# A hybrid encoder block on one core: the input projection spread over the steps of attention and mLSTM, and attention's scores with keys on partitions

## The chip, the cores and the metric

The kernel runs on one core of a Trainium2 chip (trn2). The metric is device microseconds of one execution. Engines are named as the profile names them: PE (TensorE, matmuls; PEld its weight loads), DVE (VectorE), ACT (ScalarE), POOL (GpSimd), SP (SyncE, which here only starts DMAs). Each engine runs its own instructions strictly in order and waits at semaphores, so an instruction that waits holds everything behind it on its engine.

## The reference, cut to what matters

One encoder layer with the same weights on two requests of 512 and 1024 tokens, all in float32:

```
h = rmsnorm(x, norm_mix_pre)                                  # (tokens, 1024)
z = h @ w_in                                                  # D_IN = 512+128+128 + 4*512 + 16 + 2*1024
aq, ak, av, mq, mk, mv, mo, gate_pre, ga, gm = split(z)
a = axial_gqa(aq, ak, av)   # 8 q heads, 2 kv heads of 64; rmsnorm and rotary on q, k; softmax over keys
m = bidir_mlstm(mq, mk, mv, mo, gate_pre)   # 4 heads of 128, forward and backward
merged = sigmoid(ga) * (a @ w_attn_o) + sigmoid(gm) * (m @ w_mlstm_o)
x = x + rmsnorm(merged @ w_out)
y = x + rmsnorm((gelu(conv3(u_gate)) * u_val) @ w_down)       # u = rmsnorm(x) @ w_up
```

With keys s and queries q, attention is softmax(q k^T / 8) v. The mLSTM of a head and a direction is computed as weights W[s, t] = exp(a_s + negA_t) (k_s . q_t), masked to one side of the diagonal, numerators W^T v, denominators the sum of W over s.

## The kernel before, in words

The two requests lie one behind the other: 1536 tokens, 12 tiles of 128 (`NT`), 3 chunks of 512 (`NCH`); chunk 0 is the first request, chunks 1 and 2 the second (`SEG_OF_CHUNK`). Every product is made of three matmuls on operands split into a high and a low part (`mm3`, L75: high x high, low x high, high x low), so a weight or an activation must first be split: a copy into the high part and a subtraction into the low part. "A matmul" below moves 512 columns unless said otherwise.

The kernel is a row of stages, each a block with its own tiles and semaphores, with a barrier of all engines between two. The order within an engine is the order of the code; loops are mostly hardware loops (`Fori`).

1. `norm_and_qkv`: rmsnorm, transpose to `hT_hi`, `hT_lo` (features on partitions, both kept in SBUF for all tokens), the 768 columns of attention's q, k, v, their norm and the rotation on POOL. q and k (transposed) and v go to DRAM unsplit.
2. `input_projection`: 33 tiles of 128 output columns (the gates first), each 3 chunks x 8 contraction tiles x 3 matmuls = 72 matmuls (L534 to L540). A weight tile is loaded once, split by DVE (L470, L472), and serves all three chunks. ACT evacuates, with Sigmoid where mo, ga and gm need it (L568), and stores to `zT` in DRAM. The gates' scans run on DVE in between.
3. `attention`: 4 pairs of heads, each 24 units of 128 queries. Scores are made with queries on partitions (L874, L875: 128 queries x 512 keys), DVE takes the row extreme (L820), ACT the exponential with its sum (L761), DVE normalises (L833), PE transposes the probabilities (L886: 640 transposes), ACT and DVE split them (L771, L842), PE multiplies by v (L898, L900).
4. `mlstm`: 4 heads, 20 steps of (chunk, key tile) and 32 items (step, direction) each. Per item ACT makes the decays (L1083, L1087), DVE multiplies with the scores (L1139), ACT and DVE split (L1095, L1145), PE adds to the numerators `pMN` (L1245 to L1247) and, with a full 128x128 stationary of ones, to the denominators `pMD` (L1248, L1249). At the end of a chunk DVE picks the diagonal of `pMD` (L1154, L1159).
5. `mlstm_norm`, `merge`, `out_projection`, `ffn`, `final_norm`.

## Time and profile before

| | us |
|---|---|
| median of 3 runs | 2899.56 (2897.19 to 2907.11) |
| span of the profiled execution | 2895.6 |
| PE busy in it | 2523.8 (87%) |
| DVE / ACT / POOL busy | 1602.1 / 792.8 / 237.2 |
| DMA | 177.45 MB, mean 61 GB/s |

The profiled execution is known by its span alone; the median of the runs lies 4.0 us above it.

The stages, by the first and last instructions of each: norm and q/k/v from 0 to about 200 us; input projection, first matmul 208.3, last 749.7; attention, first matmul 775.0, last 1097.6; mLSTM, first score 1116.2, last instruction 1394.4; its norm until the first matmul of the merge at 1444.5; then merge, output projection, feed-forward network and last norm until 2895.6.

How to read it: an engine's busy time is the union of its instructions; a matmul's own duration (390 ns) overlaps the next, so the price of one more matmul is the distance between two starts, not its duration. `PEclk` and the column before the DMA share in a table of stretches is TensorE's granted clock as a share of 2.4 GHz (0.50 is 1.2 GHz). "Idle before, releaser" says how long the engine stood before a group of instructions and what ended it.

### The profile page before, as it was taken

To read this page: it belongs to the slowest core of one execution; us is meant where nothing else is said; L and a number is where in the kernel's file an instruction comes from. 1 tells how busy PE (TensorE), PEld (TensorE's weight loads), DVE (VectorE), ACT (ScalarE), POOL (GpSimd) and SP (SyncE) were. 2 spreads that over 40 slices of the span, in tenths; PEclk is the share of its full clock that TensorE was granted. 3 is DMA by queue.
4 is the path that set the end of the run, shared out by engine and by line. 5 is a ranking of instruction groups with operands and counts; after the bars stand their busy time and mean duration, and the time that the engine had idled before them with its cause. 6 is when DMAs were issued, how large, how long until landed. Compare 5 with 4: busy or idle time off the path is not lost. (4 is left out here: it accounts for less than half of the span.)

```text
span 2895.6 us, 35416 instructions
## 1 busy us (share of the span) xinstructions
PE 2523.8 (87%) x11484; PEld 2056.6 (71%) x11484; DVE 1602.1 (55%) x2319; ACT 792.8 (27%) x1384; POOL 237.2 (8%) x245
## 2 busy tenths in 40 slices
PE   4859999999687886778397997999999999999993
PEld 3758888888455654656386785888888888888882
DVE  4631122111388985777733663666666565757577
ACT  2311211111377675555300232111111111111113
POOL 1530000000111111111222000000000000000000
PEclk9989999999799998999699998999999999999996
DMA  3221222222200003210243532011101010111004
GB/s 108 80 49 62 86 78 78 86 73 76 71 17 0 11 0 93 60 58 8 84 161 138 176 123 65 24 37 29 36 29 36 29 36 29 36 29 36 29 15 181
DMA packets 153542, 177.45 MB, mean 61 GB/s; under 512 B 15497, under 2 KB 123273, under 8 KB 153489
## 3 DMA queue, kind: packets, MB, share of 16 engines
q1 hardware_dynamic: 134528, 133.09, 15.1%
q10 hardware_dynamic: 18960, 43.72, 4.2%
q8 instruction: 25, 0.41, 0.1%
q14 instruction: 29, 0.23, 0.0%
HBM read 127.97 MB, written 48.81 MB: 61 GB/s over the span
## 5 line engine op out<-in xcount | busy, mean ns | idle before, releaser
L77 PE MATMUL pZ<-hT_hi,win_hi 128*128 128x512 f32 x792 | 309.2, 390 | 15.9 <-DVE win_lo L472 15.9
L78 PE MATMUL pZ<-hT_hi,win_lo 128*128 128x512 f32 x792 | 308.9, 390 | 0.0
L79 PE MATMUL pZ<-hT_lo,win_hi 128*128 128x512 f32 x792 | 308.8, 390 | 0.0
L1874 DVE TENSOR_TENSOR y_sum<-y_sum,pVal 128x512 f32<-128x512 f32 x252 | 171.6, 687 | 208.8 <-PE pVal L79 208.8
L470 DVE CAST win_hi<-win_raw 128x1024 fp32r<-128x1024 f32 x33 | 22.9, 694 | 430.7 <-PE pZ L79 425.7
L77 PE MATMUL pG<-h2T_hi,wg_hi 128*128 128x512 f32 x528 | 206.6, 391 | 11.6 <-DVE wg_lo L1821 11.6
L78 PE MATMUL pG<-h2T_hi,wg_lo 128*128 128x512 f32 x528 | 206.2, 391 | 0.0
L79 PE MATMUL pG<-h2T_lo,wg_hi 128*128 128x512 f32 x528 | 206.2, 390 | 0.0
L79 PE MATMUL pVal<-h2T_lo,wv_hi 128*128 128x512 f32 x528 | 205.4, 389 | 0.0
L78 PE MATMUL pVal<-h2T_hi,wv_lo 128*128 128x512 f32 x528 | 205.4, 389 | 0.0
L77 PE MATMUL pVal<-h2T_hi,wv_hi 128*128 128x512 f32 x528 | 205.4, 389 | 0.0
L77 PEld LDWEIGHTS pZ<-hT_hi,win_hi 128*128 128x128 f32 x792 | 149.2, 188 | 47.1 <-DVE win_lo L472 16.3
L568 ACT ACTIVATE z_st<-pZ 128x512 f32<-128x512 f32 x96 | 57.3, 598 | 450.2 <-PE pZ L79 450.2
L1874 DVE TENSOR_TENSOR y_sum<-y_sum,pD 128x512 f32<-128x512 f32 x252 | 172.3, 688 | 0.3 <-PE pD L79 0.3
L78 PEld LDWEIGHTS pZ<-hT_hi,win_lo 128*128 128x128 f32 x792 | 149.1, 188 | 31.2
L79 PEld LDWEIGHTS pZ<-hT_lo,win_hi 128*128 128x128 f32 x792 | 149.1, 188 | 31.0
L1919 ACT ACT_TABLE_LOAD x22 | 28.2, 1283 | 477.1 <-DVE conv L1854 477.1
L886 PE MATMUL pAT<-ident,probs 128*128 128x128 f32 x640 | 103.8, 294 | 39.3 <-DVE pT_lo L842 29.2
L886 PEld LDWEIGHTS pAT<-ident,probs 128*128 128x128 f32 x640 | 72.5, 146 | 86.0 <-DVE pT_lo L842 64.3
L77 PEld LDWEIGHTS pG<-h2T_hi,wg_hi 128*128 128x128 f32 x528 | 99.6, 189 | 32.7 <-DVE wg_lo L1821 12.0
L78 PEld LDWEIGHTS pG<-h2T_hi,wg_lo 128*128 128x128 f32 x528 | 99.7, 189 | 20.8
L79 PEld LDWEIGHTS pG<-h2T_lo,wg_hi 128*128 128x128 f32 x528 | 99.6, 189 | 20.8
(240 smaller groups left out, 5553.8 us busy)
## 6 DMA issues: line engine op xcount, KB each, us to landing
zT_scratch<-z_st ACTq DMA_DIRECT2D x32, 768.0 KB, 3.6
ffn_raw<-in_w_up SPq DMA_DIRECT2D x44, 512.0 KB, 3.8
win_raw<-in_w_in SPq DMA_DIRECT2D x32, 512.0 KB, 4.1
a_T<-zT_scratch SPq DMA_DIRECT2D x16, 768.0 KB, 8.5
ffn_raw<-in_w_down SPq DMA_DIRECT2D x22, 512.0 KB, 4.4
x_t<-in_x SPq DMA_DIRECT2D x12, 512.0 KB, 3.4
negA_rows<-negA_scratch SPq DMA_DIRECT2D x24, 256.0 KB, 5.1
mergedT_scratch<-h_sum ACTq DMA_DIRECT2D x8, 768.0 KB, 8.8
```

The costliest lines, as they stand in the source:

```text
L77: pe.matmul(out, w_hi, x_hi, start=first, stop=False, **kw)
L78: pe.matmul(out, w_lo, x_hi, start=False, stop=False, **kw)
L79: return pe.matmul(out, w_hi, x_lo, start=False, stop=last, **kw)
L470: dve.tensor_copy(w_hi[:, b], raw[:, b]).then_inc(hi_done, 1)
L568: act.activation(dst[:, c * CH:(c + 1) * CH], pZ[:, b, c, :], func).then_inc(bank_free, 1)
L886: last = pe.transpose(pT[:, at % 2, i, :], probs[:, u % 2, kt * P:(kt + 1) * P], k.ident[:, :])
L1874: dve.tensor_tensor(y_sum[:, t, cols], y_sum[:, t, cols], down_bank(2 * t + h), ALU.add).then_inc(summed, 1)
L1919: act.activation(gelu[:, :], conv[:, :], ACT.Gelu_apprx_tanh, bias=b).then_inc(gelu_done, 1)
```

## The change

The stage `input_projection` is gone. What it did is now spread:

- the 16 gate columns are 16 more columns of the q/k/v product (`WQ`), padded, transposed and kept in `gates`;
- the high and low parts of h go to DRAM and are read back in pieces of 128x512; q, k and v go to DRAM already split;
- the 12 tiles of mq, mk, mv are computed within attention and the 20 tiles of mo, ga, gm within mLSTM, by a class `Projection`. Its order is chunk by chunk, and within a chunk tile by tile, so each weight tile is loaded and split three times (36 and 60 times). A unit is one `mm3`; 288 units are spread over attention's 84 slots, 480 over mLSTM's 128 items. ACT makes the high part of a weight tile, DVE the low part. mo, ga and gm are stored unsquashed; their Sigmoid is taken by ACT in `mlstm_norm` and `merge`.
- attention works on 24 units of (kv head, chunk, q head) with 512 queries, 80 steps of two key tiles. A first product with queries on partitions (`piece`, 160 matmuls into the single bank `pM`) serves only for the row maximum, which enters the scores as one more contraction row; the scores have keys on partitions, so no probability is transposed. POOL adds the unnormalised exponentials up over the steps (128x1024 each), DVE folds and splits that sum, PE sums it over the partitions by matmuls with two columns, and the result is divided out of the output of 64x512 per unit. Attention's result goes to DRAM and comes back in `mlstm_norm`.
- in mLSTM the decay is multiplied in place, POOL adds the weights up per chunk, and the denominators are 16 matmuls of two columns per chunk in place of two matmuls per item.
- loops are written out, and semaphores are no longer started at one.

```
-        with ExitStack() as first:
-            hT_hi, hT_lo = (sb(first, f"hT_{s}", [P, KD, TOK], F32R) for s in ("hi", "lo"))
-            clear(nc, norm_and_qkv(nc, k, hT_hi, hT_lo))
-            clear(nc, input_projection(nc, k, hT_hi, hT_lo))
-            attention(nc, k)
+            clear(nc, norm_and_qkv(nc, k))
+            clear(nc, attention(nc, k))
+            clear(nc, mlstm(nc, k))
...
+class Projection:
+    RAW, OUT = 2, 4
...
+    def high(self, act, g):
+        act.wait_ge(self.w_in[g % 2], 16 * (g // 2 + 1))
+        if g >= 2:
+            act.wait_ge(self.product, g - 1)
+        act.activation(self.w_hi[:, g % 2], self.raw[:, g % 2], ACT.Copy).then_inc(self.hi_done, 1)
+    def low(self, dve, g):
+        dve.wait_ge(self.hi_done, g + 1)
+        dve.tensor_tensor(self.w_lo[:, g % 2], self.raw[:, g % 2], self.w_hi[:, g % 2].bitcast(F32),
+                          ALU.subtract).then_inc(self.split, 1)
+    def keep(self, act, g):
+        act.wait_ge(self.product, g + 1)
+        act.activation(self.z_st[:, g % self.OUT, :], self.pZ[:, g % 2, :], ACT.Copy).then_inc(self.kept, 1)
+    def unit(self, pe, x):
+        g, kt = divmod(x, KD)
...
+        done = mm3(pe, self.pZ[:, b, :], self.w_hi[:, b, kt, :], self.w_lo[:, b, kt, :],
+                   self.h_hi[:, s, :], self.h_lo[:, s, :], kt == 0, kt == KD - 1)
...
 def attention(nc, k):
+    fill = Projection(nc, ctx, sem, k, "_a", list(range(3 * MH)), 12)
+    # POOL
+            for i, (u, s) in enumerate(STEPS):
+                pool.wait_ge(exped, i + 1)
+                if s == 0:
+                    pool.tensor_copy(acc[:, u % 2, :], probs[:, i % 2, :]).then_inc(added_up, 1)
+                else:
+                    pool.tensor_tensor(acc[:, u % 2, :], acc[:, u % 2, :], probs[:, i % 2, :], ALU.add).then_inc(added_up, 1)
+    # DVE, one slot i
+                for u in ending(i - 1): invert(u)
+                keep_lo(i + 1)
+                for u in ending(i - 1): normalise(u)
+                for u in ending(i): fold(u)
+                for g in ended_before(i): fill.low(dve, g + 2)
+                for u, p in PIECES[i + LEAD]: reduce(u, p)
...
+    # PE, one slot i
+                project(due - 2 * (due // 3))
+                for u in ending(i - 1): turn_inverse(u)
+                for u in starting(i + 3): turn_top(u)
+                weigh(i)
+                project(due // 3)
+                scores(i + 2)
+                for u, p in PIECES[i + LEAD][:half_done]: piece(u, p)
+                project(due // 3)
+                for u, p in PIECES[i + LEAD][half_done:]: piece(u, p)
+                for u in ending(i): sums(u)
...
 def mlstm(nc, k):
+    fill = Projection(nc, ctx, sem, k, "_m", list(range(3 * MH, 4 * MH + 2 * KD)), 10)
-                    pe.matmul(pD[:, d, cols], ones[:, :], hi, start=first, stop=False, **free)
-                    pe.matmul(pD[:, d, cols], ones[:, :], lo, start=False, stop=True, **free).then_inc(weighed, 1)
+    # POOL, per item x
+            pool.tensor_tensor(w_sum[:, j % 2, d, cols], w_sum[:, j % 2, d, cols], w_all[:, x % RING, cols],
+                               ALU.add).then_inc(added_up, 1)
+    # PE, one item x
+                    project(due - due // 2)
+                    if FIRST[t] == x and t + 2 < NS * MH: scores(t + 2)
+                    weigh(x)
+                    project(due // 2)
+                for j in after(x, SUMS): denominators(j)
...
 def mlstm_norm(nc, k):
+                act.wait_ge(o_in[h % 2], 16 * (h // 2 + 1))
+                act.activation(sig_o[:, h % 2, :], sig_o[:, h % 2, :], ACT.Sigmoid).then_inc(o_ready, 1)
+                act.wait_ge(a_in[h], 16)
```

PE in attention, before, in the steady part: `pS` are scores, `pAT` transposed probabilities, `pO` the output.

```order
L874 MATMUL pS<-k_hi,q_stack 128x512 [waits exped]
L875 MATMUL pS<-k_lo,q_stack 128x512
L874 MATMUL pS<-k_hi,q_stack 128x512
L875 MATMUL pS<-k_lo,q_stack 128x512
L883 REGISTER_ALU [waits normed]
L886 MATMUL pAT<-ident,probs 128x128 [waits pT_lo_done]
L886 MATMUL pAT<-ident,probs 128x128 x3
```

PE in attention, now, one slot of a unit of eight key tiles: `pZ_a` is the projection, `pM` the bank of the row maximum.

```order
L970 MATMUL pO<-p_hi,v_both 128x512 [waits p_lo_done]
L971 MATMUL pO<-p_lo,v_both 128x512
L970 MATMUL pO<-p_hi,v_both 128x512
L971 MATMUL pO<-p_lo,v_both 128x512
L77 MATMUL pZ_a<-hT_hi_a,win_hi_a 128x512
L78 MATMUL pZ_a<-hT_hi_a,win_lo_a 128x512
L79 MATMUL pZ_a<-hT_lo_a,win_hi_a 128x512
L955 MATMUL pS<-q_stack,k_stack 128x512 [waits exped]
L956 MATMUL pS<-q_max,k_low 128x512
L955 MATMUL pS<-q_stack,k_stack 128x512
L956 MATMUL pS<-q_max,k_low 128x512
L938 MATMUL pM<-k_stack,q_stack 128x512 [waits k_in1,q_in0,reduced,m_kept,o_normed]
```

The transposes and their wait for the normalised probabilities are gone; each slot carries scores, products with v, one or two pieces into `pM`, and projection between them, and a piece waits until the one before it is reduced.

DVE in attention, now, the slots around the end of a unit: `p_lo` the low part of the probabilities, `p_fold` the folded sum, `win_lo_a` the low part of a weight tile, `att_top` the reductions of `pM`.

```order
L814 TENSOR_TENSOR p_lo<-probs,p_hi 128x1024 [waits p_hi_done]
L819 TENSOR_TENSOR p_fold<-p_sum 128x512 [waits p_added]
L823 CAST p_fold_hi<-p_fold 128x512 [waits p_summed,p_folded]
L825 TENSOR_TENSOR p_fold_lo<-p_fold,p_fold_hi 128x512 [waits fold_hi]
L497 TENSOR_TENSOR win_lo_a<-win_raw_a,win_hi_a 128x1024 [waits win_hi_done]
L801 TENSOR_REDUCE att_top<-pM 128x1 [waits pieced] x2
L831 TENSOR_TENSOR o_sum<-pO,o_half 64x512 [waits o_normed,o_halved]
L835 RECIPROCAL att_rinv<-pM 128x4 [waits p_summed]
L839 TENSOR_TENSOR att_rwide<-att_wide,att_rinv 128x512 [waits r_turned,inverted]
L814 TENSOR_TENSOR p_lo<-probs,p_hi 128x1024 [waits p_hi_done]
L847 TENSOR_TENSOR o_out<-o_sum,pM 64x512 [waits a_out0,o_added,r_turned]
```

None of these rows stood there before; the reductions that free `pM` for PE stand behind the subtractions that read two SBUF tiles.

PE in mLSTM, before, two items of a chunk: `pMN` numerators, `pMD` denominators.

```order
L1245 MATMUL pMN<-mw_hi,mv_hi 128x256 [waits w_lo_done]
L1246 MATMUL pMN<-mw_lo,mv_hi 128x256
L1247 MATMUL pMN<-mw_hi,mv_lo 128x256
L1248 MATMUL pMD<-mw_hi,m_ones 128x256
L1249 MATMUL pMD<-mw_lo,m_ones 128x256
L1245 MATMUL pMN<-mw_hi,mv_hi 128x384 [waits w_lo_done]
```

PE in mLSTM, now, where a chunk has ended: `pMV<-m_ones` are the first of the 16 short matmuls of the denominators.

```order
L77 MATMUL pMS<-mq_hi,mk_hi 128x512 [waits multiplied,m_split]
L78 MATMUL pMS<-mq_hi,mk_lo 128x512
L79 MATMUL pMS<-mq_lo,mk_hi 128x512
L1448 MATMUL pMN<-mw_hi,mv_hi 128x512 [waits copied_f,v_split,w_lo_done]
L1449 MATMUL pMN<-mw_lo,mv_hi 128x512
L1450 MATMUL pMN<-mw_hi,mv_lo 128x512
L77 MATMUL pZ_m<-hT_hi_m,win_hi_m 128x512 [waits z_kept,win_split]
L78 MATMUL pZ_m<-hT_hi_m,win_lo_m 128x512
L79 MATMUL pZ_m<-hT_lo_m,win_hi_m 128x512
L1460 MATMUL pMV<-m_ones,w_sum_hi 128x2 [waits w_sum_split]
L1461 MATMUL pMV<-m_ones,w_sum_lo 128x2
```

The two `pMD` matmuls per item have gone; a wait for `w_sum_split` (POOL's sum and two DVE splits of it) stands in the row of matmuls once a chunk.

## Rows read from the trace of the kernel before

**Rows 1.** The page: busy time of the engines; one group
```profile
PE 2523.8 (87%) x11484; PEld 2056.6 (71%) x11484; DVE 1602.1 (55%) x2319; ACT 792.8 (27%) x1384; POOL 237.2 (8%) x245
...
L1919 ACT ACT_TABLE_LOAD x22 | 28.2, 1283 | 477.1 <-DVE conv L1854 477.1
```

**Rows 2.** Stretches: length; PE, PEld, DVE, ACT, POOL busy; clock, DMA share, GB/s
```profile
0.00:208.00 208.00, 130.68 (x732) 112.02 (x732) 108.34 (x131) 52.67 (x98) 78.35 (x83) 0.91 0.25 75
208.00:752.00 544.00, 542.65 (x2400) 448.76 (x2400) 82.32 (x81) 72.42 (x109) 0.00 (x0) 1.00 0.24 76
752.00:1105.00 353.00, 261.58 (x1280) 187.93 (x1280) 285.49 (x455) 230.04 (x417) 63.99 (x38) 0.91 0.06 18
1105.00:1394.00 289.00, 214.88 (x1024) 174.04 (x1024) 216.31 (x411) 162.32 (x376) 47.89 (x96) 0.91 0.19 55
1394.00:1440.00 46.00, 11.28 (x48) 9.68 (x48) 34.51 (x21) 19.42 (x17) 16.17 (x4) 0.50 0.21 71
```

**Rows 3.** Timeline of PE: start us, us, instruction; projection, then transposes
```profile
749.24 0.39 PE L77 MATMUL pZ<-hT_hi,win_hi 128*128 128x512 f32 x1
749.46 0.39 PE L78 MATMUL pZ<-hT_hi,win_lo 128*128 128x512 f32 x1
...
750.01 0.96 PE L545 MATMUL pGate<-ident,gate_t 64*128 64x64 f32 x12
...
1407.73 2.82 PE L1407 MATMUL pNT<-ident,m_hn 128*128 128x128 f32 x12 [17.22 <-DVE m_hn L1368]
```

**Rows 4.** Stretch of attention in its steady part
```profile
870.00:880.00 10.00, 8.36 (x47) 6.02 (x47) 9.89 (x16) 7.31 (x13) 0.00 (x0) 1.00 0.00 0
```

**Rows 5.** Groups by line, 208 to 1394: busy us, mean ns | idle before, releaser
```profile
L820 DVE TENSOR_REDUCE att_small<-pS 128x1 f32<-128x512 f32 x32 | 21.9, 684 | 8.3 <-PE pS L875 7.8
L472 DVE TENSOR_TENSOR win_lo<-win_raw,win_hi 128x1024 fp32r<-128x1024 f32 x33 | 40.4, 1225 | 1.1
L761 ACT ACTIVATE probs<-pS,att_small 128x1024 f32<-128x1024 f32 x64 | 71.3, 1114 | 3.4 <-DVE att_small L820 3.4
L478 DVE TENSOR_TENSOR_SCAN gate_cum<-gate_ones,gf 32x1024 f32<-32x1024 f32 x1 | 2.3, 2279 | 0.0
```

**Rows 6.** Groups by line, whole span, mLSTM's
```profile
L1145 DVE TENSOR_TENSOR mw_lo<-w_all,mw_hi 128x512 fp32r<-128x512 f32 (+3 forms) x128 | 70.2, 548 | 6.0 <-ACT mw_hi L1095 5.4
L1139 DVE TENSOR_TENSOR w_all<-decay,pMS 128x512 f32<-128x512 f32 (+3 forms) x128 | 68.1, 534 | 25.8 <-PE pMS L79 12.2 <-issue 5.3 <-ACT decay L1087 4.3
L1248 PE MATMUL pMD<-mw_hi,m_ones 128*128 128x512 f32 (+3 forms) x128 | 45.9, 359 | 0.0
```

**Rows 7.** One line, POOL: ns least/median/most, first and last start
```profile
L717 POOL TENSOR_TENSOR v_both<-v_raw,v_both x2: 1803/2562/3321, 771.4 to 936.8; 128x768 fp32r<-128x768 f32 x2
```

**Rows 8.** Timeline of DVE and POOL in the norm after mLSTM
```profile
1405.91 1.76 DVE L1368 TENSOR_TENSOR m_hn<-h_sum,m_stat 128x1536 f32<-128x1536 f32 x1
...
1422.97 3.42 POOL L1348 TENSOR_TENSOR branch_lo<-a_T,branch_hi 128x1536 fp32r<-128x1536 f32 x1 [1.58 <-ACT branch_hi L1339]
1423.18 4.83 DVE L1368 TENSOR_TENSOR m_hn<-h_sum,m_stat 128x1536 f32<-128x1536 f32 x1
```

**Rows 9.** Timeline of PE: the first matmul of each stage, and one chunk's end
```profile
208.32 0.80 PE L77 MATMUL pZ<-hT_hi,win_hi 128*128 128x512 f32 x1 [15.89 <-DVE win_lo L472]
...
775.03 0.79 PE L874 MATMUL pS<-k_hi,q_stack 128*128 128x512 f32 x1 [24.06 <-DVE q_stack L665]
...
1116.16 0.79 PE L77 MATMUL pMS<-mq_hi,mk_hi 128*128 128x512 f32 x1 [1.87 <-DVE mq_lo L1127]
...
1233.79 0.50 PE L1245 MATMUL pMN<-mw_hi,mv_hi 128*128 128x512 f32 x1 [2.56 <-DVE floor_c L1159]
...
1444.48 0.79 PE L77 MATMUL pB<-branch_hi,wbo_hi 128*128 128x512 f32 x1 [13.60 <-DVE wbo_lo L1475]
```

**Rows 10.** Timeline of DVE at the start of the program
```profile
32.22 0.56 DVE L237 CAST wqkv_hi<-gates 128x768 fp32r<-128x768 f32 x1 [10.07 <-DMA gates<-in_w_in]
```

**Rows 11.** Stretch at the start of mLSTM, when its tiles are loaded
```profile
1110.00:1120.00 10.00, 4.93 (x13) 3.37 (x13) 3.92 (x6) 4.18 (x10) 3.01 (x6) 0.50 1.01 341
```

More of the change, by code:

```diff
@@ L55 @@
 COL_GA = COL_GATE + N_GATE
[L56 removed]
+Q_SCALE = HEAD ** -0.5
 NEG = -1.0e30
@@ new lines, in sums, with turn_inverse @@
+            def sums(u):
+                pe.wait_ge(fold_split, u + 1)
+                for qb in range(4):
+                    cols = slice(qb * P, (qb + 1) * P)
+                    pe.matmul(pM[:, 2 * qb:2 * qb + 2], s_hi[:, cols], ones[:, :], start=True, stop=False)
+                    last = pe.matmul(pM[:, 2 * qb:2 * qb + 2], s_lo[:, cols], ones[:, :], start=False, stop=True)
+                last.then_inc(summed, 1)
+            def turn_inverse(u):
+                pe.wait_ge(widened, u + 1)
+                for qb in range(4):
+                    last = pe.transpose(pM[:, qb * P:(qb + 1) * P], rwide[:, qb, :], k.ident[:, :])
+                last.then_inc(r_turned, 1)
@@ L1000, in cut, with chunk @@
+        FIRST_WAY = {}
+        for x, (n, m) in enumerate(ITEMS):
+            FIRST_WAY.setdefault((NCH * n + STEPS[ONE[m][0]][0], ONE[m][1]), x)
+        DUE = units_by_slot(fill.units, len(ITEMS))
+        ENDS = fill.ends(DUE)
         def cut(c):
             return slice(c * CH, (c + 1) * CH)
[L1003 to L1014 removed]
+        def chunk(x):
+            n, m = ITEMS[x]
+            return NCH * n + STEPS[ONE[m][0]][0]
@@ L1283, in _, with project, prepare @@
-            prepare(0, 0)
-            heads(pe, head)
+            done = [0]
+            def project(n):
+                for x in range(done[0], done[0] + n):
+                    fill.unit(pe, x)
+                done[0] += n
+            def prepare(j):
+                n, c = divmod(j, NCH)
+                b = j % 2
+                pe.wait_ge(raw_in[b], 48 * (j // 2 + 1))
+                if j:
+                    pe.wait_ge(v_split, j)
+                divided = sum(1 for y in range(NCH * MH) if last_of(y) + TURN <= ready_at[j])
+                if divided:
+                    pe.wait_ge(scaled, 2 * divided)
+                for a in range(4):
+                    last = pe.transpose(pV[:, 0, a, :], raw[:, b, 2, a * P:(a + 1) * P], k.ident[:, :])
+                last.then_inc(v_turned, 1)
@@ new lines, in denominators @@
+            def denominators(j):
+                pe.wait_ge(sum_split, j + 1)
+                if j:
+                    pe.wait_ge(scaled, 2 * j)
+                for d in range(2):
+                    for b in range(4):
+                        out = pV[:, 1, 0, 2 * (4 * d + b):2 * (4 * d + b) + 2]
+                        cols = slice(b * P, (b + 1) * P)
+                        pe.matmul(out, s_hi[:, d, cols], ones[:, :], start=True, stop=False)
+                        last = pe.matmul(out, s_lo[:, d, cols], ones[:, :], start=False, stop=True)
+                last.then_inc(den_done, 1)
@@ L1288, in mlstm_norm @@
+    return used
 def mlstm_norm(nc, k):
```

1888 lines of the change are left out of this document (1030 added, 858 removed).

## Prediction, made before the changed kernel was run

> **What bounds the kernel now.** I read the page first, then a table of stretches cut at the stages, then the timeline of PE for the price of a matmul, then the groups by line, last the timelines where a stage begins. PE is busy 87% of the span [rows 1], so the question is where it isn't, and where it does work that goes away. The input projection is pure PE: 542.65 of 544 us at clock 1.00, while DVE works 82 us and ACT 72 [rows 2]. Attention is the reverse: PE 262 of 353 us, DVE 285; in its steady part DVE is busy 9.89 of 10 us and PE 8.36 [rows 4], so DVE sets the pace. mLSTM has PE at 215 of 289 and DVE at 216 [rows 2], its gaps at the ends of chunks (PE stood 2.56 us for the picked denominators in [rows 9]). Laying the first stage's matmuls into the gaps of the other two is worth at most what PE idles there, 91 + 74 us, plus the hand-over between two stages (749.7 to 775.0, 25 us, most of it the 24.06 us before the first score [rows 9]), plus PE work that goes.
>
> **Prices.** Two matmuls of 512 columns start 0.22 to 0.23 us apart [rows 3]; over the whole projection 542.65 us by 2376 such matmuls and 24 small ones give 0.2275 [rows 2]. A 128x128 transpose is 2.82 / 12 = 0.235 us, a 64x64 one 0.96 / 12 = 0.08 [rows 3]. DVE: 0.68 us for 512 columns out of PSUM, 1.225 for a subtraction of 1024 columns [rows 5].
>
> **The change, part by part**, on the profiled execution (span 2895.6; the median of the runs is 4.0 above it, which I add at the end).
>
> *Until attention runs.* The first projection matmul stood at 208.3 [rows 9]. With four buffers for the q/k/v weights DVE no longer stands 10.07 us for the third tile [rows 10]; between 0 and 10 I take 8 off. Sixteen more columns (24 matmuls x 16/512 x 0.2275 = 0.17 us) and one more transpose (0.235) per tile cost 0.4 x 12 = 5 us; DVE loses two copies per tile and gains two smaller subtractions, nothing. Then attention's first slot: DVE subtracts two weight tiles before its loop, and the second one stands on SP behind 16 loads of h of 256 KB and some 2 MB of q, k and weights, about 6 MB; at the 341 GB/s of [rows 11] that is 18 us against the few that one weight tile took. In the meantime PE has only two or three units. I take +10 (bounds 0 and 18). Attention runs freely from 208 - 8 + 5 + 10 = 215.
>
> *Attention, PE's work.* 160 pieces, 320 matmuls of scores, 320 with v, 288 units x 3 = 864 of projection: 1664 x 0.2275 = 379 us. 192 transposes 45. The 192 matmuls of two columns are in no row: between 0 and a transpose's 0.235 (45 us); I take the 64x64 row, 0.08, 15 us. Sum 439, of which 197 is projection; the old work of this stage was 262, so 20 us go. At clock 1.00: [rows 4] has it there with 84% busy.
>
> *Attention, DVE's work.* 80 subtractions of 1024 columns 98 us; 160 reductions at 0.684, 109; 36 low parts of weights 44; per unit two additions, two subtractions or copies, a widening, a normalisation and a reciprocal, about 3.9 us x 24 = 95; the gates' scans, which used to lie in DVE's idle time, 20 (four long ones of 2.28 [rows 5], four of half the length, four plain passes). 366 us, under PE's 439: PE becomes the bound if DVE is never late.
>
> *What is late next.* Within a slot PE needs 2.34 (projection) + 0.91 + 0.91 + 0.46 = 4.62 us. `pM` is one bank: the second piece waits until DVE has reduced the first, and DVE has the subtraction of the next step and often a weight's low part in front. The length of that chain after a score: exponential 1.1 [rows 5], POOL's add, subtraction 1.2, reduction 0.7; it has two slots to fit, 9.2 us, so it is hidden in a plain slot. It isn't at a unit's end: fold, copy and subtraction (some 1.8 us) stand before the reductions, `sums` waits for them, `turn_inverse` waits for DVE's widening. I take 3 us of PE standing for each of the 16 long units and 2.5 for each of the 8 short ones, 68 us, from the chunk ends of mLSTM before (2.56 [rows 9]); bounds 0 and 6 us each (144). Attention takes 439 + 68 = 507 and ends at 722.
>
> POOL: an add of 1024 columns is in no row; 768 took 1.80 us undisturbed [rows 7], so 2.4 us. 56 adds 134 us and 24 copies at half of it 29: 163 us, far below the stage's 507, and each has two slots. What it does to DVE is seen in [rows 8]: a multiplication of two SBUF tiles took 1.76 us by itself and 4.83 beside a POOL subtraction that ran from 1422.97 to 1426.39; 4.83 is the 3.21 us left of it plus 1.62. So DVE waited for the whole of POOL's instruction. The subtraction `p_lo` of a step becomes ready about 1 us after POOL's add of that step has begun, and waits up to 1.4 us. In plain slots the slack above takes that; with more of it see the second rival.
> The Trainium skill (SBUF — State Buffer, section "SBUF: two separate sides") says that the port pair which VectorE and GpSimd share is locked for a whole instruction, by a VectorE instruction with two SBUF inputs among others, and that the loser blocks fully. Row 4.83 agrees. By that rule alone every one of the 80 steps could lose 2.4 us.
>
> *Attention to mLSTM.* Before, 1097.6 to 1116.2, 18.6 us [rows 9]. Now the same barrier and loads, and again 16 loads of h before the second weight tile; +10, as above: 28, mLSTM runs freely from 750.
>
> *mLSTM, PE's work.* 480 units, 1440 matmuls, 328 us; 240 of scores 55; three products per item in place of five. The 128 items have 47104 columns, so 3 x 92 = 276 full matmuls, 63 us (the two that go, those of ones [rows 6], are 42 us); 144 transposes 34; 192 short ones 15. Sum 495, 3.9 us per item. DVE has 68 + 70 [rows 6] + 60 low parts at 1.225 = 74 + about 95 for chunks and heads = 307, POOL about 120 for its adds, 48 for masks [rows 2] and 10 for clearing: even one after the other, 485, they stay under PE. DVE and ACT can be two items ahead, so plain items are hidden. At the 12 chunk ends PE waits for POOL's sum and two DVE passes over 1024 columns (0.7 + 1.2): again 3 us each, 36 (bounds 0 and 72), and the last chunk's tail is 8. 539, to 1289.
>
> *Norm and merge.* 1394.4 to 1444.5, 50 us. On ACT now four Sigmoids of 1536 columns (1.5 each) with a change of table to and fro (2 x 1.28 a head [rows 1]), behind 4.7 MB of loads at the start; partly on DVE's chain. +10 (bounds 0 and 20). Merge's eight Sigmoids lie on an ACT that was idle; +2 for the first. From 1444.5 to 2895.6 the rest is untouched, 1451.
>
> Sum: 1289 + 50 + 10 + 1451 + 2 = 2802 less 4 for the units done before the loops run freely, 2798 of span; with the 4.0 us, **2802 us**, 3.4% faster. Its own range is 2750 to 2860.
>
> **Rivals.**
> *PE never waits.* If two slots of slack also cover the unit and chunk ends, 68 + 36 go, and the first loads cost nothing (20): 2802 - 104 to 124, about 2690. For it: DVE 366 against PE 439, 307 against 495. Against it: before, with plainer chains, PE stood a quarter of both stages [rows 2].
> *POOL's adds hold DVE up* (the other side). Place: `p_lo` in attention. If no POOL instruction overlaps useful DVE work, DVE's stage is 366 + 163 = 529 us, 6.3 us a slot over PE's 5.2, and the unit ends come on top, 24 x 3.5 = 84: 613 in place of 507, and 10 or so more in mLSTM's starts: 2802 + 106 + 10 = 2918, slower than before. It decides from some 7.3 us a slot on. For it: the 4.83 us of [rows 8]; against it: 109 of DVE's 366 us are reductions from PSUM in which POOL can run, and a late DVE finds POOL already done.
> *The clock.* Short stalls could cost more than themselves if the granted clock fell from 1.00 to 0.50 (2.4 to 1.2 GHz), as it does in the hand-over of [rows 11]. At a mean of 0.87 over PE's 934 us: +140, 2940. Against it: 1.00 in [rows 4] with PE at 84%.
> That the change doesn't do what it says is no case: the units stand between the other matmuls in PE's program.
>
> **How the numbers follow.** Forecast 0.55; PE never waits, or nearly (under 2750), 0.20; POOL holds DVE up, wholly or in part (over 2860), 0.20; clock 0.05. Of the third two thirds still end below before. Below 2891 (faster by over 0.3%, which is what a measurement of this kernel can tell from no change): 0.55 + 0.20 + 0.12 = 0.87; within it 0.03; slower 0.10. The range that leaves out 2 in 10: 2710 to 2895.
>
> **What would show it.** Projection matmuls between those of scores and of v; attention's PE busy near 439 us in a stage of about 507, mLSTM's near 495 in about 540; clock near 1.00 in both. In attention the piece's line should stand for the reduction a second or so per slot at most, and most of PE's idle time should lie before `sums`, `turn_inverse` and `turn_top`. `p_lo` should show a median above 1.225 us, up to 2.6; if it is near 3.6 and DVE is busy above 95%, the second rival is right. In mLSTM the idle time should lie before the two-column matmuls; if it lies in plain items, my two items of lead are wrong. Wrong would also be a first free slot much after 215, or a stage of the merge that moves by more than a few us.

## The result, and the profile after

| | median of the runs | span of the profiled one |
|---|---|---|
| before | 2897.85 us (2895.79 to 2907.11) | 2895.6 us |
| changed | 2909.43 us (2904.86 to 2916.7) | 2904.2 us |

The ratio is 1.0038, with a 95% interval from 1.0027 to 1.0048: 0.4% slower, where 2802 us, 3.4% faster, was forecast. The page's busy line answers to [rows 1]:

```profile
PE 2535.9 (87%) x11264; PEld 2060.5 (71%) x11264; DVE 1717.6 (59%) x2333; ACT 879.3 (30%) x1315; POOL 512.0 (18%) x430
```

PE has 220 instructions less than before and 12 us more of busy time. The stretches (length; PE, PEld, DVE, ACT, POOL busy; granted clock, DMA share, GB/s) are cut where attention runs freely, where it ends, where mLSTM runs freely and where it ends; they answer to [rows 2].

```profile
0.00:217.00 217.00, 137.17 (x762) 117.24 (x763) 96.45 (x137) 56.26 (x124) 73.34 (x85) 0.88 0.68 192
217.00:844.00 627.00, 513.36 (x2034) 385.55 (x2033) 394.71 (x466) 256.62 (x286) 167.61 (x80) 0.89 0.27 78
844.00:867.00 23.00, 4.99 (x34) 3.99 (x34) 4.37 (x10) 3.24 (x8) 2.27 (x5) 0.53 0.61 200
867.00:1394.00 527.00, 503.90 (x2392) 418.78 (x2390) 312.68 (x479) 249.19 (x492) 223.09 (x232) 0.97 0.46 136
1394.00:1451.00 57.00, 11.52 (x49) 9.93 (x50) 35.56 (x22) 34.56 (x28) 14.79 (x4) 0.56 0.37 136
```

| us | forecast | measured |
|---|---|---|
| until attention runs freely | 215 | 217 |
| attention | 507 | 627 |
| hand-over to mLSTM | 28 | 23 |
| mLSTM | 539 | 527 |
| norm after it | 60 | 57 |
| merge to the end | 1453 | 1453 |

Five of the six terms are within 12 us. The time misses by 107 us; attention alone misses by 120, and the other terms give some of it back. PE is idle there for 114 us (68 forecast), and it is busy for 513 where the work was priced at 439 us of full clock; the granted clock of the stage is 0.89, not 1.00. PE's waits in that stretch (us in total, times, longest):

```profile
PE pM L938 <- DVE att_top L801: 56.3, 28, 7.7
PE pM L944 <- DVE att_tops L810: 16.8, 14, 1.5
PE pM L979 <- DVE att_top L801: 14.1, 18, 0.8
PE pM L938 <- DVE att_tops L799: 13.4, 5, 4.0
PE pM L986 <- DVE att_rwide L839: 4.3, 8, 1.6
PE pM L979 <- DVE att_tops L799: 3.1, 4, 0.8
```

L938 is the piece, L979 `sums`, L944 `turn_top`, L986 `turn_inverse`. 70 of these 108 us lie at the piece and 38 at the other three, where most of the waiting was expected; all of them are at the one bank `pM`. The longest, in the timeline (start us, us, instruction, in brackets the idle time before it and what ended it):

```profile
393.31 0.40 PE L938 MATMUL pM<-k_stack,q_stack 128*128 128x512 f32 x1
394.80 2.28 DVE L855 TENSOR_TENSOR_SCAN gate_t<-gate_ones,gate_gi 32x1024 f32<-32x1024 f32 x1
395.19 4.03 POOL L719 TENSOR_TENSOR p_sum<-p_sum,probs 128x1024 f32<-128x1024 f32 x1 [5.07 <-ACT probs L728]
397.11 3.19 DVE L814 TENSOR_TENSOR p_lo<-probs,p_hi 128x1024 fp32r<-128x1024 f32 x1
400.22 1.21 DVE L497 TENSOR_TENSOR win_lo_a<-win_raw_a,win_hi_a 128x1024 fp32r<-128x1024 f32 x1
401.35 0.68 DVE L801 TENSOR_REDUCE att_top<-pM 128x1 f32<-128x512 f32 x1
402.08 0.79 PE L938 MATMUL pM<-k_stack,q_stack 128*128 128x512 f32 x1 [7.69 <-DVE att_top L801]
402.68 0.63 PE L77 MATMUL pZ_a<-hT_hi_a,win_hi_a 128*128 128x512 f32 x1
```

The piece of 393.31 was done at 393.7. Its reduction, 0.68 us, began at 401.35, behind a scan, a `p_lo` of 3.19 us that ran into GpSimd's add, and the low part of a weight. DVE is busy for 63% of this stage and still late here: the instruction PE needs stands behind the rest of its slot. Ahead of the wait a matmul of 512 columns shows 0.40 us, behind it 0.63 (the clock is at its lower level).

The loss isn't spread evenly. The first line is 20 slots of long units (eight key tiles), the second 8 slots of short ones (four):

```profile
417.70:556.60 138.90, 118.87 (x490) 89.95 (x489) 91.95 (x106) 59.59 (x67) 42.08 (x20) 0.92 0.40 113
556.60:635.70 79.10, 63.20 (x228) 46.69 (x226) 41.71 (x60) 26.88 (x31) 15.75 (x8) 0.78 0.19 52
```

A slot takes 9.9 us in the short units, at a clock of 0.78, and 6.9 in the long ones. mLSTM, by contrast, shows what was expected and less; its waits, 867 to 1394:

```profile
PE pMS L77 <- DVE w_all L1328: 7.6, 1, 7.6
PE pMV L1460 <- DVE w_sum_lo L1344: 5.8, 7, 1.3
PE pZ_m L77 <- DMA hT_lo_m<-hT_lo_scratch: 3.0, 2, 2.6
```

The 12 chunk ends cost 5.8 us together, not 36. The firsts that answer to [rows 9]:

```profile
194.83 0.77 PE L77 MATMUL pZ_a<-hT_hi_a,win_hi_a 128*128 128x512 f32 x1 [20.05 <-DVE win_lo_a L497]
211.56 0.80 PE L938 MATMUL pM<-k_stack,q_stack 128*128 128x512 f32 x1 [13.40 <-DVE att_tops L799]
857.00 1.09 PE L1423 MATMUL pMV<-ident,m_raw 128*128 128x128 f32 x4 [11.46 <-DMA m_raw<-zT_scratch]
1450.77 0.79 PE L77 MATMUL pB<-branch_hi,wbo_hi 128*128 128x512 f32 x1 [16.55 <-DVE wbo_lo L1696]
```

### The profile page after: what moved, and what is told of

Read it like the earlier page. It is cut to its first block and busy times, and to the rows that moved or that the text cites. A ratio compares the mean times of both kernels' runs of the same rounds, so it can differ in the third digit from the quotient of the medians.

```text
span 2904.2 us, 33464 instructions
## 1 busy us (share of the span) xinstructions
PE 2535.9 (87%) x11264; PEld 2060.5 (71%) x11264; DVE 1717.6 (59%) x2333; ACT 879.3 (30%) x1315; POOL 512.0 (18%) x430
## 5 line engine op out<-in xcount | busy, mean ns | idle before, releaser
L77 PE MATMUL pZ_m<-hT_hi_m,win_hi_m 128*128 128x512 f32 x480 | 196.0, 408 | 9.5 <-DVE win_lo_m L497 6.6
L1223 POOL TENSOR_TENSOR w_sum<-w_sum,w_all 128x512 f32<-128x512 f32 (+3 forms) x128 | 149.5, 1168 | 291.5 <-DVE w_all L1328 262.0
L719 POOL TENSOR_TENSOR p_sum<-p_sum,probs 128x1024 f32<-128x1024 f32 x56 | 142.2, 2539 | 312.2 <-ACT probs L728 312.2
L78 PE MATMUL pZ_m<-hT_hi_m,win_lo_m 128*128 128x512 f32 x480 | 190.6, 397 | 0.0
L79 PE MATMUL pZ_m<-hT_lo_m,win_hi_m 128*128 128x512 f32 x480 | 190.6, 397 | 0.0
L497 DVE TENSOR_TENSOR win_lo_m<-win_raw_m,win_hi_m 128x1024 fp32r<-128x1024 f32 x60 | 84.9, 1415 | 137.1 <-ACT win_hi_m L493 137.1
L938 PE MATMUL pM<-k_stack,q_stack 128*128 128x512 f32 x160 | 76.8, 480 | 88.3 <-DVE att_top L801 56.3
L814 DVE TENSOR_TENSOR p_lo<-probs,p_hi 128x1024 fp32r<-128x1024 f32 x80 | 117.7, 1471 | 59.3 <-ACT p_hi L734 59.2
L801 DVE TENSOR_REDUCE att_top<-pM 128x1 f32<-128x512 f32 x128 | 88.3, 690 | 103.4 <-PE pM L938 103.4
L77 PE MATMUL pZ_a<-hT_hi_a,win_hi_a 128*128 128x512 f32 x288 | 126.7, 440 | 20.1 <-DVE win_lo_a L497 20.1
L78 PE MATMUL pZ_a<-hT_hi_a,win_lo_a 128*128 128x512 f32 x288 | 122.6, 426 | 0.0
```

The lines of the kernel that those rows point to most:

```text
L77: pe.matmul(out, w_hi, x_hi, start=first, stop=False, **kw)
L78: pe.matmul(out, w_lo, x_hi, start=False, stop=False, **kw)
L79: return pe.matmul(out, w_hi, x_lo, start=False, stop=last, **kw)
L497: dve.tensor_tensor(self.w_lo[:, g % 2], self.raw[:, g % 2], self.w_hi[:, g % 2].bitcast(F32), ALU.subtract).then_inc(self.split, 1)
L719: pool.tensor_tensor(acc[:, u % 2, :], acc[:, u % 2, :], probs[:, i % 2, :], ALU.add).then_inc(added_up, 1)
L801: dve.tensor_reduce(top2[:, qb, s:s + 1], pM[:, :], AX_X, ALU.max).then_inc(reduced, 1)
```

## Experiments

Theory A: PE stands at the one bank `pM`, because the reductions stand last in DVE's slot, and each wait is paid about twice, once as idle time and once as half clock. Its rivals, by turns: B, GpSimd's adds hold DVE up; the clock falls for a reason of its own; the waits belong to PE's own chain, wherever they show. All edits are in attention (e16 to e18 move a load in mLSTM as well). Each ratio is to the kernel before, run beside it; the changed kernel stands at 1.0038.

| kernel | median us | ratio, 95% interval |
|---|---|---|
| e1_low_last | 2895.4 | 0.9989 (0.9978 to 1.0001) |
| e2_scans_spread | 2906.8 | 1.0037 (1.0022 to 1.0053) |
| e3_between | 2885.7 | 0.9956 (0.9940 to 0.9973) |
| e4_apart | 3105.1 | 1.0713 (1.0696 to 1.0731) |
| e5_reorder | 2872.3 | 0.9900 (0.9880 to 0.9919) |
| e6_pool_two_columns | 2875.4 | 0.9910 (0.9893 to 0.9926) |
| e7_filler | 2911.5 | 1.0044 (1.0027 to 1.0061) |
| e8_apart_filler | 3075.9 | 1.0607 (1.0589 to 1.0625) |
| e9_two_banks | 2811.9 | 0.9694 (0.9678 to 0.9711) |
| e10_apart_two_banks | 3072.4 | 1.0601 (1.0583 to 1.0618) |
| e11_adds_on_dve | 2871.9 | 0.9905 (0.9888 to 0.9921) |
| e12_scans_too | 2814.5 | 0.9709 (0.9693 to 0.9725) |
| e13_one_bank_again | 2851.3 | 0.9843 (0.9827 to 0.9859) |
| e14_late_sums | 2883.8 | 0.9947 (0.9929 to 0.9966) |
| e15_fold_first | 2859.7 | 0.9866 (0.9850 to 0.9882) |
| e16_weights_first | 2853.4 | 0.9837 (0.9821 to 0.9854) |
| e17_best_weights_first | 2809.4 | 0.9691 (0.9676 to 0.9707) |
| e18_fold_elsewhere | 2792.9 | 0.9638 (0.9622 to 0.9653) |

### What stands ahead of the reduction: e1, e2, e3

```diff
 # e1, DVE's slot
+for u, p in PIECES[i + LEAD]: reduce(u, p)
+for u in starting(i + 4): top(u)
 for g in ended_before(i): fill.low(dve, g + 2)
-for u, p in PIECES[i + LEAD]: reduce(u, p)
-for u in starting(i + 4): top(u)
 # e2: the scans at n = 1 and n = 3, four each, become one each at n = 1 to 4 and 6 to 9
 # e3, PE's slot (due is 3 or 4)
-project(due - 2 * (due // 3)); ...; weigh(i); project(due // 3); scores(i + 2); piece; project(due // 3); piece
+project(due - due // 3 - due // 2); ...; weigh(i); scores(i + 2); piece; project(due // 2 + due // 3); piece
```

> Attention only: in every slot DVE makes the low part of a projection weight (36 of them, 1.2 to 1.5 us each) after the reductions of pM, not before them. Theory A (PE stands at pM because the reductions are late behind other DVE work, and the granted clock falls to 0.50 where it stands): about half of the 56 us at the pieces lies in slots with a low part, so 20 to 30 us of standing go and 10 to 20 us of half clock with them: 2865 to 2880. Theory B (the clock falls for another reason, or the pieces wait for PE's own chain): less than 5 us.

> Attention only: the eight gate scans of DVE, which ran four at a time in two slots, run one at a time in eight slots. Theory A: the waits of up to 7.7 us between 330 and 400 us go, 10 to 15 us of standing and 10 to 15 of half clock (granted clock of 340 to 380 from 0.8 to about 1.0): about 2885. Theory B: under 5 us.

> Attention only, PE's order: the projection unit that stood between weigh and scores, and one of those ahead of weigh, stand between the two pieces of a slot (2 or 3 units of 0.68 us there, in place of 1). Theory A: the second piece finds the reduction of the first one done in nearly every slot, while the first piece of the slot comes no later than before; 20 to 40 us of standing go, with half clock 30 to 70: about 2855. Theory B: under 5 us. A rival to both: the scores, now without a unit ahead of them, wait more for the exponentials, and it comes out slower.

e1 gives 14 us (0.5% less than the changed kernel), e3 24, e2 nothing: all three fell short of what was expected. In e1 the wait of the pieces for `att_top` falls from 56 to 41 us. Reductions that come late behind DVE's work are on the path, but each single edit gives less than its waits promise. In e2 the clock from 340 to 380 us rises from 0.80 to 0.91, but the waits at the pieces add up to 55 us as before. In e3 the waits at the pieces stay (56.6 us at L938 for `att_top`), though they were to go; the stage (217 to 820) has 498 us of PE busy and 105 idle, for 513 and 114. So the mechanism was not the one expected; where the 24 us come from was not found.

### Without the projection between: e4, e8, e10

```diff
+APART = 24
-LEAD = 4
+LEAD = 4 + APART
-DUE = units_by_slot(fill.units, NS + LEAD)
+DUE = [fill.units // APART] * APART + [0] * (NS + 4)
 # e8 adds, ahead of each piece
+for _ in range(2): pe.matmul(fill.pZ[:, g % 2, :], nil, wide_ones, ...)      # nil is zero
 # e10 in place of that: pieces alternate between pM and fill.pZ[:, 0, :]
-if at: pe.wait_ge(reduced, at)
+if at: pe.wait_ge(reduced, at - (at > 4))
```

> The same attention, but its 288 projection units run in 24 slots of their own ahead of it (12 a slot, still with ACT's and DVE's work for them), none between its steps. Projection alone is 288 x 0.68 = 197 us at full clock. Attention without it has 242 us of PE work and, by the trace, about 350 us of DVE work. If laying the units between the steps is worth what PE would stand without them, attention alone takes 400 us or more and this kernel is at least as slow as the changed one (2905 or more). If the interleaving itself costs (units that delay scores, reductions and exponentials), attention alone takes under 400 us and the kernel comes out at 2870 or so. The forecast's arithmetic (PE is the bound at 507 us together) would say 197 + 400 to 430, 100 us slower than 507 but near the 626 measured.

> The kernel with the projection apart (3105 us; attention alone 605 us at a mean granted clock of 0.67, where PE has 242 us of work at full clock), with two matmuls of zero weights ahead of each of the 160 pieces: 73 us more of PE work. If the low clock is what makes attention alone as long as attention with the projection in it, the clock rises above 0.8 and the stage gets shorter than 605, 500 to 580 us, the kernel 3000 to 3080. If the stage's length comes from its chains of waits at any clock, it gets longer by 40 to 70 us: 3145 to 3175.

> The kernel with the projection apart (3105 us, attention alone 605), where the pieces alternate over pM and a bank of the projection's, which is free there; nothing else is changed. If the single bank is what makes attention alone 7.5 us a step at 60% of DVE, at least 0.6 us a step and the half clock that goes with it go: 3000 to 3050. If it is the rest of the chain (scores, exponential, high part, subtraction, and the unit ends), under 20 us: 3085 or more.

Attention alone (the stretch after the last unit), of e4, e8 and e10, one line of each kernel:

```profile
434.00:1039.00 605.00, 402.73 (x1187) 291.34 (x1186) 358.03 (x431) 204.15 (x214) 167.52 (x80) 0.66 0.09 22
```

```profile
434.00:1009.00 575.00, 399.20 (x1505) 292.79 (x1504) 354.63 (x432) 206.32 (x217) 166.53 (x80) 0.85 0.09 24
```

```profile
434.00:1003.00 569.00, 351.38 (x1164) 269.62 (x1163) 390.10 (x428) 204.11 (x214) 168.02 (x80) 0.74 0.09 24
```

With the 288 units taken out, attention still takes 605 us against 627 with them: all but 22 of the 197 us of projection are hidden, as forecast, but inside a stage that is itself slow. The stage of before, with queries on partitions, took 353 [rows 2]. Its new order is bounded neither by PE's work (242 us at full clock) nor by DVE's (358 of 605). e8 shows the clock at work: 320 matmuls more, 73 us of work at full clock, and the stage is 30 us shorter, at a clock of 0.85 in place of 0.66. PE's busy time is the same (403 and 399 us) with that work added; its idle time falls from 202 to 176. e10 gives the pieces a second bank; its stage is 36 us shorter and the kernel 33 us faster, less than the 55 that were the least expected: PE now waits 90 us at `sums` (for reductions) and 46 at `turn_top`, 17 and 32 in e4.

### The clock in the changed kernel: e7

```diff
 def piece(u, p):
+    filler(2)      # two matmuls of zero weights into the open projection group
```

> The changed kernel with two matmuls of zero weights by 512 columns ahead of every piece (wherever a projection group is open: about 280 of them, which add nothing to the result). 64 us of PE work at full clock, of which a third to a half should lie in PE's waits at the pieces. If the granted clock falls because PE stands or is thinly used there, it rises from 0.89 to 0.95 or more in attention, some 40 us or more of half clock go, and the kernel is no slower than without the fillers: 2885 to 2915. If the clock doesn't follow PE's activity, it is 30 to 50 us slower: 2940 to 2960.

Some 60 us of PE work more, and the kernel is not slower beyond the scatter (1.0044 against 1.0038). The stage's clock went from 0.89 to 0.93, not to the 0.95 expected; over the same 627 us PE is busy for 547 in place of 513 and idle for 80 in place of 114. So about half of the added work lay in waits and the other half came back by the higher clock; fillers gain nothing here.

### GpSimd: e6, e11

```diff
 # e6 (its sums lack all later steps but two columns)
-pool.tensor_tensor(acc[:, u % 2, :], acc[:, u % 2, :], probs[:, i % 2, :], ALU.add)
+pool.tensor_tensor(acc[:, u % 2, 0:2], acc[:, u % 2, 0:2], probs[:, i % 2, 0:2], ALU.add)
 # e11, on e5: the same adds and copies as dve.tensor_tensor and dve.tensor_copy, behind top(u)
```

> GpSimd's 56 adds of 1024 columns in attention work on 2 columns only (the sums of the exponentials lack the later steps; the first step's copy adds 1.0). Rival B (the adds hold DVE up at p_lo): p_lo goes from a mean of 1471 to 1225 ns, 20 us over 80, and with the waits of PE behind it and their half clock the kernel gains 40 to 60 us: 2850 to 2865. Theory A (DVE's order, not POOL): DVE is free 37% of the stage, so the gain is 20 us at most, 2885 to 2905.

> The reordered kernel (2872 us) with the adds of the exponentials, 56 adds of 1024 columns and 24 copies, on DVE behind the reductions; GpSimd does nothing in attention. Without GpSimd p_lo should fall to 1225 ns from 1324, 8 us, and DVE gets 56 x 1.22 + 24 x 0.7 = 85 us of work more, 460 of 590 us. Rival B (GpSimd's adds hold DVE up by their port): no slower, 2855 to 2875. Theory A (what counts is what stands ahead of the reductions in DVE's order): 10 to 40 us slower, 2882 to 2912.

e6 gains 1.3%, 37 us: more than theory A allowed, a little less than the rival's 40. DVE's busy time in the stage falls from 395 to 353 us (217 to 815). The subtraction `p_lo` is only half of that, 20 us (its mean falls from 1471 to 1221 ns); 16 are the 16 maxima of four columns in `top`. Two lines' instructions (ns least/median/most), of the changed kernel and of e6:

```profile
L810 DVE TENSOR_TENSOR att_tops<-att_top x16: 167/1246/1680, 282.8 to 808.9; 128x4 f32<-128x4 f32 x16
L814 DVE TENSOR_TENSOR p_lo<-probs,p_hi x80: 1209/1225/3190, 228.9 to 836.2; 128x1024 fp32r<-128x1024 f32 x80
```

```profile
L810 DVE TENSOR_TENSOR att_tops<-att_top x16: 165/166/167, 285.0 to 779.5; 128x4 f32<-128x4 f32 x16
L814 DVE TENSOR_TENSOR p_lo<-probs,p_hi x80: 1209/1222/1228, 228.2 to 804.3; 128x1024 fp32r<-128x1024 f32 x80
```

A maximum of four columns, 0.17 us by itself, takes 1.25 us as the median beside the adds, and it is the one `turn_top` waits for (16.8 us in the list above, 3.4 in e6). One of them in the changed kernel, with the add beside it:

```profile
807.81 2.36 POOL L719 TENSOR_TENSOR p_sum<-p_sum,probs 128x1024 f32<-128x1024 f32 x1 [9.46 <-ACT probs L728]
808.95 1.25 DVE L810 TENSOR_TENSOR att_tops<-att_top 128x4 f32<-128x4 f32 x1
```

It ends at 810.20, just behind the add's 810.17. That agrees with the rule of the Trainium skill that the prediction cited (SBUF — State Buffer, section "SBUF: two separate sides"), by which the later one blocks until the earlier one's instruction has ended. The gain of e6 is idle time of PE alone: 86 us in place of 114, at the same 0.89 of clock and 512 us of busy time. e11 puts the adds on DVE: 56 of 1.22 us and 24 of 0.68, 85 us of work, for 27 us more of busy time (427 against 400 over 217 to 810), and the kernel takes the same time as e5. Moving the adds to GpSimd gained nothing here: by these figures some 58 of the 85 us it takes off DVE come back as longer DVE instructions.

### Order and banks together: e5, e9, e13

```diff
 # e5 = e1 + e3, and on ACT keep_hi(i + 1) ahead of keep_top(u)
 # e9 = e5, and:
+bank(at) = pM if at % 2 else pM2          # pieces; sums and turn_inverse use pM2
-if at: pe.wait_ge(reduced, at)
+if at >= 2: pe.wait_ge(reduced, at - 1)
+fill = Projection(..., banks=1)           # pZ has one bank; groups end at a slot's end,
+                                          # 4+4 or 3+3+2 units; ACT: exp, keep(g), keep_hi
+weigh(i) at the head of PE's slot; add_halves behind the first reduction
 # e13 = e9 with every piece, sums and turn_inverse in pM, and the old waits
```

> Attention only, three changes of order together: the low part of a weight after the reductions on DVE (that alone gave 11 us), two or three projection units between the two pieces of a slot (that alone gave 21), and on ACT the high part of the exponentials ahead of keep_top. In the timeline ACT's high part waited 3 us behind keep_top (which waits for turn_top), so that the subtraction p_lo and, behind it, fold and the reductions came late. Theory A (late reductions): the gains add and the swap brings some 10 us more: 2865 to 2875. If the waits only move to another place: 2885, as with the units alone.

> The three changes of order that gave 2872, and in attention a second PSUM bank for the pieces (pieces alternate over two banks, so a piece waits for the reduction of the piece before the last; sums and the inverse's turn use one of the two). The bank comes from the projection's results, which have one bank here in place of two; their groups end at a slot's end, ACT takes them out right behind an exponential, and PE's slot begins with weigh to cover that. Theory A (the single bank pM and the reductions in it are what PE stands for): of the 43 + 18 us at the pieces and 19 at sums in the reordered kernel 50 us or more go, and 20 us or more of half clock with them: 2800 to 2830. Rival (PE's slots are held up by whatever comes next on DVE and ACT, the single projection bank among it): the waits turn up at the projection's first matmul and at weigh, and the gain is under 15 us: 2860 or more.

> The same kernel (2812) with all pieces in the one bank pM again, each waiting for the reduction of the one before it, and sums behind the last reduction; the slot's order, the projection's single bank and its whole groups stay. Theory A (the single bank): most of the 60 us between the reordered kernel (2872) and this one come back, 2855 to 2875. Rival (the order of the slot did it, weigh first above all): 2812 to 2825.

Waits of PE in attention, e9 (217 to 747), then e13 (217 to 786):

```profile
PE pM L987 <- DVE att_top L805: 22.2, 10, 4.8
PE pO L978 <- DVE p_lo L818: 13.7, 5, 6.8
PE pM L994 <- DVE att_rwide L843: 11.3, 10, 2.2
...
PE pM L946 <- DVE att_top L805: 2.0, 3, 0.8
```

```profile
PE pM L946 <- DVE att_top L805: 49.7, 24, 7.6
PE pM L987 <- DVE att_top L805: 14.1, 18, 0.8
```

e9 takes 2812 us, 3.1% under before; attention is 530 us at a clock of 0.93, and the pieces' wait for `att_top`, 56 us in the changed kernel and 43 in e5, is 2 us. Given back the single bank alone, e13 loses 39 us and has 49.7 us of that wait again. So of the 60 us from e5 to e9 the bank is 39; the other 21 are e9's other edits together (the order of the slot, whole groups, one projection bank). e5 itself gave the 40 us against the changed kernel that were expected of it.

A wait's total is not its price. PE in attention, from 217 us to the end of the stage:

| kernel | stage | PE idle | PE busy | clock |
|---|---|---|---|---|
| changed | 627 | 114 | 513 | 0.89 |
| e6_pool_two_columns | 598 | 86 | 512 | 0.89 |
| e13_one_bank_again | 570 | 81 | 489 | 0.90 |
| e9_two_banks | 530 | 64 | 466 | 0.93 |
| e18_fold_elsewhere | 510 | 62 | 448 | 0.95 |

From e13 to e9 the 48 us that go at the pieces are 17 of idle time, as other waits grow, and 23 of busy time, at a higher clock. The short units gained most: their 16 slots take 154 us in the changed kernel, 124 in e13 and 106 in e9, that is 48 of the 97 us between the changed kernel and e9 in a fifth of the slots.

### Moving what is left: e12, e14, e15, e16, e17, e18

```diff
 # e12 = e9 + e2
 # e14 = e12, sums(u) behind the next slot's weigh, turn_inverse behind its scores, fold behind the reductions
 # e15 = e14 with fold ahead of the reductions again
 # e16 = e15, e17 = e9: fill.load_w(sp, 1) ahead of the 16 loads of h, in both stages
 # e18 = e17, and fold's three passes: the add on GpSimd, the high part on ACT, the low part on DVE
```

> The kernel with two banks for the pieces (2812 us) with the eight gate scans one at a time, the edit that gave nothing on the changed kernel. There PE still waits 6.8 and 6.0 us at weigh for p_lo behind the scans, with 4.2 and 4.9 us at sums, and the granted clock is 0.83 from 300 to 380. If what one late step costs depends on what else is late, the edit is now worth 10 to 25 us: 2787 to 2802. If it is worth nothing here either (under 3 us), the scans were never on the path.

> The kernel with two banks and spread scans, with the sums of a unit and the turn of its inverse one slot later: sums behind the next slot's weigh, turn_inverse behind its scores, and DVE's fold behind the reductions. In the kernel with two banks PE waits 22 us at sums and 11 at turn_inverse, and has half clock behind some of them. If these waits only need other work ahead of them, 20 to 30 us go against the kernel with the scans spread: 2765 to 2780. If DVE, which has 386 us of work in 523, is late anyway, under 8 us.

> The kernel with sums and turn_inverse one slot later (2884), with fold ahead of the reductions again. Theory A' (each wait of PE costs itself and about as much again, whatever the engine that is late; fold behind the reductions was 51 us of it): the waits at sums fall under 10 us, 2765 to 2800, faster than with sums in their old place (2814). If the late sums themselves are the fault (pO and pM2 come free later, normed later), 2830 or more.

> The same as e15_fold_first, with the second weight tile asked for ahead of the 16 loads of h, in attention and in mLSTM. In the trace PE stands 11 to 12 us at about 210 for a reduction that lies behind DVE's subtraction of that tile, and 7 us at about 768. If the tile's place on SP is the cause, 10 to 18 us less than e15_fold_first; if the loads' sum (6 MB at 341 GB/s) is, the same within 3 us.

> The kernel with two banks for the pieces (2812), and the second weight tile asked for ahead of the 16 loads of h. That edit gave 6 us on the kernel with late sums (2860 to 2853), where its waits of 11.5 us became 9.7 + 5.0 for the h tiles themselves. The same here: 2804 to 2809. If its gain there was within the scatter: 2810 to 2814.

> The same with two of fold's three passes off DVE: GpSimd adds the two halves behind its last add of a unit, ACT makes the high part, DVE keeps the subtraction (0.69 us of 1.8) and makes it behind the first reduction of the slot. If DVE's load at the unit's end sets PE's waits there, the 22 us at sums fall to about 10 and half clock with them, 15 to 25 us faster than e17_best_weights_first: 2780 to 2792. If the wait only moves on to the next late step (the sum of the two halves, or turn_inverse), as it did with the late sums: within 5 us of it.

e12 gains nothing again, although the two waits of 6.8 and 6.0 us behind scans are gone: where two waits of over 4 us stood at sums there are now five of 3.8 to 4.7. The scans' work is the same and comes out of the same slots; how it is packed made no difference. e14 missed by 100 us and e15 by 60. The largest wait of each, e14, then e15:

```profile
PE pM L990 <- DVE p_fold_lo L829: 51.0, 22, 3.8
```

```profile
PE pO L981 <- DVE o_sum L835: 49.5, 19, 5.4
```

With sums one slot later PE waits for other late work of DVE: first fold, then the halves' sum, for which the next unit's first `weigh` waits. My reading, which no run tests by itself, is that DVE's work at a unit's end was late for the next slot anyway. e16 is 6 us faster than e15 and e17 2 us than e9, with intervals that overlap: the place of the second weight tile is worth 0 to 10 us; the wait of 11.5 us for it turns into one of 9.7 for `q_max`. e18 takes 1.1 us of the unit's end away from DVE, makes what is left of fold behind the first reduction, and gains 17 us on e17 (0.9638 against 0.9691), as expected. PE's wait at sums falls from 22 to 9.5 us, also as expected, but those for `p_lo` and `att_rwide` grow (14 to 18 and 11 to 16); its idle time falls by 6 us only, from 68 to 62, and its busy time by 14. Its stage:

```profile
217.00:727.00 510.00, 447.81 (x2008) 350.81 (x2007) 377.00 (x418) 267.17 (x308) 214.80 (x104) 0.95 0.33 94
```

510 us, at a PE busy time of 448, close to the forecast's 507 and 439, but in another kernel than the one the forecast was for. e18 beats both kernels, by 3.6% the one before.

## Why the prediction was wrong

**The step that failed** is the forecast's "507": attention's 68 us of stalls at a clock of 1.00, which were 114 at 0.89. Everything else of the sum held. The mechanism (PE becomes the bound, the projection hides the gaps) was right for mLSTM, but not for this kernel's attention, where PE stands and slows down at the one bank `pM`; with two banks and a new order attention comes near it.

*"It has two slots to fit, 9.2 us, so it is hidden in a plain slot."* That is true of the exponential's chain, and PE hardly waits at `weigh`. The piece has no such slack: with one bank it has until the next piece, one projection unit (0.7 us), and the reduction takes 0.69 us and begins 0.60 us after the matmul even when DVE is free. I had listed what stands ahead of the reduction and then gave it the other chain's slack. e9 against e13 prices the bank at 39 us. A unit's pieces are also not two a slot throughout: they lie in the slots of the unit before, so where a short one precedes a long one four stand in each of its two slots; I took the mean. The first of each such two slots took 15.5 and 16.5 us (the waits of 3.8 us at 266 and 590 lie there), 10.7 and 11.0 in e13, 7.9 and 8.8 in e9 with the second bank.

*"I take 3 us of PE standing for each of the 16 long units and 2.5 for each of the 8 short ones."* The size, 68 us, was inside its bounds (0 to 144) and 46 us low. The place was wrong: 70 of 108 us stand before pieces, 17 before sums, 17 before `turn_top`, 4 before `turn_inverse`.

*"At clock 1.00: [rows 4] has it there with 84% busy."* The failed reading. Ten steady microseconds had 1.00, while the row of the whole stage in [rows 2] had 0.91, with PE at 74%. In steps of 20 us the changed kernel's attention has clocks from 0.74 to 1.00, and a stage with such waits gets the stage's value. 513 less 439 is 74 us, more than the idle time's own excess. In the kernel with the projection apart e8 shows that the clock itself costs time: more work, less time. The rival "the clock" had 0.05 of the chance and a size of 140 us for both stages; what can be put down to it is 74 us in attention and 9 in mLSTM (504 busy, 495 priced). I held it apart from the stalls, though they come together: from the changed kernel to e18 52 us of idle time go and 66 of busy time with them. That is no fixed rate: e6 took away 28 us of idle time and 1 of busy time.

*"POOL's adds hold DVE up"*, 0.20, decided from 7.3 us a slot: a slot took 627 / 80 = 7.8 us. By e6 the adds are 37 us of the miss of 120. It was not that GpSimd never overlaps DVE (DVE is busy 63%, not 95%), but that it stretches single operations on the path. `p_lo` kept its median of 1.225 us, where I expected a higher one; only its mean rose, to 1.471. In part right.

*PE's work of attention*, 439: e18 has 448 at a clock of 0.95, so by estimate 425 to 440 at full clock; right. *DVE's*, 366 against 395: 42 us of the 395 are waiting for GpSimd (e6: 353). *mLSTM*: 495 of work against 504 busy at 0.97; its chunk ends were 30 us cheaper than taken, which hides 9 us of clock and some 9 of other waits. *Until attention, hand-over, norm, merge*: 2, 5, 3 and 0 us off; the first is luck, two errors that cancel: PE ended the norm stage some 18 us earlier than before (3 were forecast), and from the first projection matmul at 194.8 to free running it took 22 us (10 forecast, bounds 0 and 18). By e16 and e17 the second tile's place is at most 10 of them.

What stays open: how the 120 us divide exactly. The parts measured one at a time (bank 39, adds 37, low parts 14, e3's order 24, e9's other edits 21) were taken on different bases and aren't independent, as e2, e12 and e14 show.

## What to carry to other kernels

Between two engines that hand one buffer to and fro, the slack is that of the buffer, not of the stage's lead: for each PSUM bank write down what its reader's engine does between the write and the read, and compare it with what the writer has to do until it needs the bank. An engine at 63% can be the one that is always late, and its order within a step is worth as much as its load. Take the granted clock from the row of the whole stage, and let a wait of PE cost about twice its length where the stage has many of them; here it was between once (e6) and 2.3 times (e13 to e9: 17 us of idle time, 40 in all).

## What the runs showed of the hardware

A stage with PE at 67% busy (e4) ran at a granted clock of 0.66, that is, for two thirds of the time at 1.2 GHz; PE at 69% busy with 320 further matmuls between its waits (e8) ran at 0.85 and finished 30 us earlier. Before, PE at 74% busy had 0.91 [rows 2]: the busy share alone doesn't tell the clock, since half clock itself makes PE busier. And a maximum of four columns on DVE took 1.25 us beside GpSimd's adds, 0.17 without them.
